# Keys, routing choice, output projection, final norm and gate weights moved beside each other in a two-layer encoder kernel on one core

## The reference, cut to what matters

```python
mem_n = rms_norm(mem, mem_norm)
for i in range(2):
    h = rms_norm(x, norm_mix[i])
    mkv = mem_n @ w_mem_kv[i]            # 1024 x 512: keys 0:256, values 256:512
    # i = 0: neighbourhood attention; i = 1: chunked gated linear attention (GLA),
    # whose decay gates come from gla_gate_up and whose output is normed by gla_out_norm
    mix, mq = ...
    x = x + concat([mix, memory_attention(mq, mkv)]) @ w_out[i]
    # top-1 of 4 groups, then top-2 of its 8 experts, each (silu(h@w1) * (h@w3)) @ w2
    x = x + hierarchical_moe(rms_norm(x, norm_ffn[i]), ...)
return rms_norm(x, final_norm)
```

## Time and profile before

| what | value |
|---|---|
| median of 3 runs | 1174.23 us (1173.82 to 1175.13) |
| the profiled execution | 1174.4 us, of which the span is 1172.6 us |
| PE busy | 875.2 us, 75% of the span |
| DVE / ACT / POOL busy | 225.5 / 181.3 / 18.6 us |
| moved by DMA | 444.06 MB, mean 379 GB/s |
| chain that ended last | PE 54%, DMA 42% |
| costliest line in it | expert weights landing, 40% |

### The profile page before, as it was taken

How to read it: one execution, slowest core, us unless ns; L and a number is a source line. 1 busy time by engine, 2 the same in 40 slices (tenths; PEclk the granted TensorE clock), 3 DMA queues, 4 the chain that set the end, 5 groups by cost and what they waited for, 6 DMA issues and landing times.

```text
span 1172.6 us, 11688 instructions
## 1 busy us (share of the span) xinstructions
PE 875.2 (75%) x5138; PEld 411.9 (35%) x5138; DVE 225.5 (19%) x427; ACT 181.3 (15%) x385; POOL 18.6 (2%) x15
## 2 busy tenths in 40 slices
PE   8999998383976465655999999976475656575676
PEld 7678553131522121211358665422121212121222
DVE  2234342010011010100115453311010101110012
ACT  3233221010000000000035521200000000000002
POOL 1400000000000000000000000000000000000000
PEclk9999999686998887877999999988787878777789
DMA  9985679999999999999999737999999999999997
GB/s 342 256 269 241 222 310 428 429 427 428 418 429 427 427 428 428 426 427 429 414 284 330 274 144 274 427 425 427 429 428 428 429 429 426 428 428 428 428 419 259
DMA packets 89769, 444.06 MB, mean 379 GB/s; under 512 B 36080, under 2 KB 54896, under 8 KB 67056
## 3 DMA queue, kind: packets, MB, share of 16 engines
q1 hardware_dynamic: 88992, 442.04, 93.5%
q10 hardware_dynamic: 720, 1.19, 0.3%
HBM read 442.16 MB, written 1.05 MB: 378 GB/s over the span
## 4 chain that ended last, share of the span: by engine, by line
PE 54%; DMA 42%; issue 1%; DVE 1%; ACT 1%; SPq 0%; DVEq 0%
DMA ring<-in_moe_w 40%; PE ps L847 15%; PE ps L851 9%; PE ps L704 5%; PE ps L1015 4%; PE ps L744 4%; PE ps L833 2%; PE ps L820 2%; PE ps L1099 2%; PE ps L752 1%; PE ps L684 1%; PE ps L697 1%; PE ps L1065 1%; PE ps L736 1%; PE ps L717 1%
## 5 line engine op out<-in xcount | busy, mean ns | idle before, releaser
L847 PE MATMUL ps<-ring,work 128*32 128x512 f32 x2032 | 274.9, 665 | 146.8 <-DMA ring<-in_moe_w 138.7
L851 PE MATMUL ps<-ring,work 128*32 128x512 f32 (+1 forms) x1088 | 141.8, 681 | 107.1 <-DMA ring<-in_moe_w 104.4
L847 PEld LDWEIGHTS ps<-ring,work 128*32 128x32 f32 x2032 | 82.1, 120 | 326.7 <-issue 326.4
L851 PEld LDWEIGHTS ps<-ring,work 128*32 128x32 f32 x1088 | 40.1, 127 | 197.7 <-issue 191.0
L1775 DVE TENSOR_TENSOR xres<-xres,ps 128x512 f32<-128x512 f32 (+1 forms) x68 | 44.6, 657 | 282.2 <-PE ps L820 282.1
L833 PE MATMUL ps<-xs,work 128*128 128x512 f32 x112 | 55.1, 638 | 10.0 <-issue 9.3
L820 PE MATMUL ps<-work 128*128 128x512 f32 (+1 forms) x136 | 59.7, 581 | 1.6 <-ACT work L1368 1.6
L1766 DVE TENSOR_TENSOR work<-work,ps 128x512 f32<-128x512 f32 x16 | 11.0, 688 | 253.2 <-PE ps L847 253.2
L704 PE MATMUL ps<-ring 128*128 128x384 f32 x160 | 53.4, 490 | 0.0
L1380 ACT COPY work<-ps 128x512 f32<-128x512 f32 x28 | 16.4, 586 | 217.8 <-PE ps L851 217.8
L1359 ACT COPY work<-ps 128x256 f32<-128x256 f32 x16 | 6.0, 372 | 268.0 <-PE ps L879 268.0
(11 more groups left out here) (254 smaller groups left out, 692.8 us busy)
## 6 DMA issues: line engine op xcount, KB each, us to landing
ring<-in_moe_w SPq DMA_DIRECT2D x187, 2048.0 KB, 31.5
ring<-in_w_out SPq DMA_DIRECT2D x4, 2048.0 KB, 16.6
ring<-in_na_w_in SPq DMA_DIRECT2D x7, 1024.0 KB, 12.2
ring<-in_gla_w_in SPq DMA_DIRECT2D x4, 1536.0 KB, 10.8
ring<-in_moe_w SPq DMA_DIRECT2D x4, 1024.0 KB, 19.6
ring<-in_moe_w SPq DMA_DIRECT2D x8, 512.0 KB, 11.4
ring<-in_na_w_in SPq DMA_DIRECT2D x1, 3072.0 KB, 19.9
ring<-in_na_rpb SPq DMA_DIRECT2D x12, 192.0 KB, 5.7
```

What stands on the lines that cost most here:

```text
L847: return pe.matmul(ps[32 * e:32 * e + 32, 4 + m, :], xsel[:, k, 32 * e:32 * e + 32], w, start=k == 0, stop=k == KC - 1, tile_position=(0, ...
L851: return pe.matmul(ps[32 * e:32 * e + 32, bank, 0:w.shape[-1]], actT[:, j, 32 * e:32 * e + 32], w, start=j == 0, stop=j == 3, tile_positio ...
```

## The change

- Layer 1's keys: their 1 MB of weights (`kw1`) is loaded by SP ahead of fill 6 of layer 0 into `work`; `mem_k(1)` runs inside quad 0 of layer 0, between the w3 products and the transposes; ACT keeps the result in `kTm1_kept` ahead of quad 0's sigmoid, and copies it to its place at quad 3. The values stay at quad 3, with a 1 MB load.
- The gates' weights go into the part of `wlog` that layer 0's logits have used, and are loaded ahead of fill 11 of layer 0; the output norm is loaded in the seam, behind w_out.
- Choice: the triangle carries -1024 on its diagonal and the ramp starts at -1024, so that `place` compares the count in PSUM itself. Both `keep_warm` matmuls stand behind L785.
- w_out of layer 1 lies in the ring as two halves by columns, not by rows, and tile 1 goes through its first half first. Slot 6 is released after that.
- The final norm's row is read once, and two matmuls with a row of ones spread it at quad 4 of layer 1.
- At the start the keys' weights come in two DMAs by halves of the rows, with a wait for each, and the memory's scaling waits for its own gain only. In the seam `vw1[0]` comes in two such halves.
- `within(0)` runs ahead of the last memory head's product.

```diff
-KV_AT = 3
+KV_AT, FNORM_AT = 3, 4
...
+CHOSEN = 1024.0
...
-    c[:, C_TRI:C_TRI + P] = np.triu(np.ones((P, P)), 1)
+    c[:, C_TRI:C_TRI + P] = np.triu(np.ones((P, P)), 1) - CHOSEN * np.eye(P)
...
-    c[:, C_IOTAM:C_IOTAM + 32] = np.arange(32) - 64
+    c[:, C_IOTAM:C_IOTAM + 32] = np.arange(32) - CHOSEN
...
-        gup = cut(ring, 10 * SLOT + 3520, 2 * DK)
+        gup = wlog[:, 0].rearrange("p k n -> p (k n)")[:, 0:2 * DK]
...
+        kw1 = cut(work, KEPT, KC, 256)
+        kTm1_kept = cut(work, 1696, MPAIR, T)
...
-        wow = [[region(0, 0, D, 4), region(6, 0, D, 4)], [region(6, 0, D, 4), region(4, 0, D, 4)]]
+        wow = [[region(0, 0, D, 4), region(6, 0, D, 4)], [region(6, 0, HALF_D, KC), region(4, 0, HALF_D, KC)]]
...
-                 2: (g_mm, 2 * TT), 7: (ring_used, B1 + 8), 10: (m_tr, 1), 8: (m_tr, 2), EXTRA: (o_mix, 2), 4: (ring_used, PRE1), 6: (ring_used, PRE1 - 1),
+                 2: (g_mm, 2 * TT), 7: (ring_used, B1 + 8), 10: (m_tr, 1), 8: (m_tr, 2), EXTRA: (o_mix, 2), 4: (ring_used, PRE1), 6: (wo_half, 2),
...
-                        sp.dma_start(kvw[1], rows(w_mem_kv[1], 0, 512)).then_inc(ring_in[kv_slot], 16)
-                        sp.wait_ge(s_gup0, 1)
-                        for dst, src in gate_loads():
-                            sp.dma_start(dst, src).then_inc(s_gate, 16)
+                        sp.dma_start(kvw[1], rows(w_mem_kv[1], 256, 512)).then_inc(ring_in[kv_slot], 16)
...
+                        if l == 0 and g == 0 and main[0].slots[f] == 7:
+                            sp.wait_ge(at_tr, N1)
+                            sp.wait_ge(s_memT, 1)
+                            sp.dma_start(kw1, rows(w_mem_kv[1], 0, 256)).then_inc(ring_in[EXTRA], 16)
+                        if l == 0 and g == 0 and f == FILLS - 1:
+                            sp.wait_ge(s_gup0, 1)
+                            for dst, src in gate_loads():
+                                sp.dma_start(dst, src).then_inc(s_gate, 16)
                         free(l, n0 + f)
...
-            sp.dma_start(kvw[0][:, :, 0:256], rows(w_mem_kv[0], 0, 256)).then_inc(ring_in[0], 16)
+            for half in range(2):
+                k = slice(4 * half, 4 * half + 4)
+                sp.dma_start(kvw[0][:, k, 0:256], rows(w_mem_kv[0], 0, 256)[:, k, :]).then_inc(ring_in[(8, 0)[half]], 16)
...
-            sp.dma_start(vw1[0][:, :, 0:HALF], chunk_rows(win1, MIX, MIX + HALF)).then_inc(ring_in[6], 16)
-            sp.dma_start(vw1[0][:, :, HALF:WIDE], chunk_rows(win1, 3 * MIX, 3 * MIX + 32)).then_inc(ring_in[6], 16)
+            for half in range(2):
+                k, there = slice(4 * half, 4 * half + 4), ring_in[(EXTRA, 6)[half]]
+                sp.dma_start(vw1[0][:, k, 0:HALF], chunk_rows(win1, MIX, MIX + HALF)[:, k, :]).then_inc(there, 16)
+                sp.dma_start(vw1[0][:, k, HALF:WIDE], chunk_rows(win1, 3 * MIX, 3 * MIX + 32)[:, k, :]).then_inc(there, 16)
...
+            sp.dma_start(gnorm, gla_out_norm[0:1, :].to_broadcast([P, DV])).then_inc(s_gate, 16)
...
-            pool.wait_ge(ring_used, PRE0 + 1)
+            pool.wait_ge(first.sel_ready, 1)
             nc.gpsimd.memset(gup, 0.0).then_inc(s_gup0, 1)
...
+            def mem_k(l):
+
...
+                w = kvw[0] if l == 0 else kw1
                 if l == 0:
-                    arrived(landed_kv0)
+                    arrived(landed_kv0[0])
                 else:
-                    slot, there = main[0].fill(0, KV_AT * FILLS)
-                    pe.wait_ge(ring_in[slot], there)
+                    arrived(landed_k1)
                     pe.wait_ge(s_memT, 1)
                 for k0 in (0, 4):
                     if l == 0 and k0 == 4:
+                        arrived(landed_kv0[1])
                         pe.wait_ge(n_hTa, TT)
                     for m in range(MPAIR):
                         for k in range(k0, k0 + 4):
-                            t = pe.matmul(ps[:, KVB[l], m * T:(m + 1) * T], w[:, k, m * P:(m + 1) * P], memT[:, k, :],
+                            t = pe.matmul(ps[:, KB[l], m * T:(m + 1) * T], w[:, k, m * P:(m + 1) * P], memT[:, k, :],
                                           start=(m, k) == (0, 0), stop=(m, k) == (MPAIR - 1, KC - 1))
                 t.then_inc(kv_mm, 1)
+
+            def mem_v(l):
...
+            def mem_v(l):
+
+                w = kvw[0][:, :, 256:512] if l == 0 else kvw[1]
...
+                else:
+                    slot, there = main[0].fill(0, KV_AT * FILLS)
+                    pe.wait_ge(ring_in[slot], there)
...
+            def out_rows(l, c, half):
+
+                if l == 0:
+                    return wow[0][c // 4][:, c % 4, HALF_D * half:HALF_D * half + HALF_D]
+                return wow[1][half][:, c, :]
...
-                keep_warm(1, NBANK[2 * l + 2][1])
+                keep_warm(2, NBANK[2 * l + 2][1])
...
-                keep_warm(2, NBANK[i][1])
                 positions1(l)
...
+                if pick_count is None and l == 0:
+                    mem_k(1)
                 pe.wait_ge(rn.sig.sel_ready, sel_count + 1)
                 for a in range(TT):
                     t = pe.transpose(ps[:, 2, a * P:(a + 1) * P], selw[:, a].rearrange("p e s -> p (e s)"), ident)
                 t.then_inc(rn.sig.selT_mm, 1)
+                if pick_count is None and l == 0:
+                    pe.wait_ge(kv_cp, 3 + 1)
                 pe.wait_ge(rn.sig.act_ready, c + 1)
...
-                        mem_kv(1)
-                        pe.wait_ge(kv_cp, 3 + 2)
+                        mem_v(1)
+                        pe.wait_ge(kv_cp, 3 + 3)
+                    if l == 1 and g == FNORM_AT:
+                        pe.wait_ge(s_fn, 16)
+                        for half in range(2):
+                            t = pe.matmul(ps[:, 2 + half, :], ones[0:1, :], fnorm[0:1, half * 512:half * 512 + 512],
+                                          start=True, stop=True)
+                        t.then_inc(s_fn, 1)
+                        pe.wait_ge(s_fn, 16 + 3)
...
-            arrived(landed_v1[0])
+            arrived(landed_v1[0][0])
             for a in range(TT):
                 for k in range(KC):
+                    if (a, k) == (0, 4):
+                        arrived(landed_v1[0][1])
...
             probs_T(N1 + 1, prob1)
+            pe.wait_ge(q_in, 2)
+            pe.wait_ge(k_in, 2)
...
+            within(0)
             pe.wait_ge(at_oT, N1 + 1)
             weighted(N1 + 1, pT1, v_mem(1, 1))
...
-            out_proj(1, 1, (0,), 5)
+            out_half(1, 0, (0, 1))
             pe.wait_ge(res[1], 1)
             transpose_tile(4, xres, 0, NBANK[4][0])
-            out_proj(1, 1, (1,), 5)
+            out_half(1, 0, (2, 3))
             logits(1, 0, range(KC))
-            out_half(1, 0, (2, 3, 4, 5)).then_inc(wo_half, 1)
+            out_half(1, 0, (4, 5)).then_inc(wo_half, 1)
+            out_half(1, 1, (0, 1))
             positions0(1)
-            second_half_of_tile1(1, (2, 3), True)
+            second_half_of_tile1(1, (2, 3))
...
-                act_e.wait_ge(kv_mm, l + 1)
-                nc.scalar.copy(kTm[l].rearrange("p m t -> p (m t)"), ps[:, KVB[l], :]).then_inc(kv_cp, 1)
                 act_e.wait_ge(ring_used, main[0].used(0, KV_AT * FILLS + 1))
-                nc.scalar.copy(vm[l].rearrange("p a n -> p (a n)"), ps[:, KVB[l] + 1, :]).then_inc(kv_cp, 1)
+                nc.scalar.copy(vm[l].rearrange("p a n -> p (a n)"), ps[:, VB[l], :]).then_inc(kv_cp, 1)
+                act_e.wait_ge(kv_cp, 3 + 1)
+                nc.scalar.copy(kTm[l], kTm1_kept).then_inc(kv_cp, 1)
+
+            def keep_k1():
+
+                act_e.wait_ge(kv_mm, 2)
+                act_e.wait_ge(first.sel_ready, 2)
+                nc.scalar.copy(kTm1_kept.rearrange("p m t -> p (m t)"), ps[:, KB[1], :]).then_inc(kv_cp, 1)
...
+                if pick_count is None and c == 0:
+                    keep_k1()
...
-                        act_e.dma_start(fnorm, final_norm.rearrange("(o d) -> o d", o=1).to_broadcast([P, D])).then_inc(s_fn, 16)
+                        act_e.dma_start(fnorm[0:1, :], final_norm.rearrange("(o d) -> o d", o=1)).then_inc(s_fn, 16)
+                    if l == 1 and g == FNORM_AT:
+                        act_e.wait_ge(s_fn, 16 + 1)
+                        for half in range(2):
+                            nc.scalar.copy(fnorm[:, half * 512:half * 512 + 512], ps[:, 2 + half, :]).then_inc(s_fn, 1)
...
-                dve.wait_ge(rt_m, 2 * l + a + 1)
-                link(V.tensor_scalar(t32a[:, a, :], msk[:, a, :], -1000.0, 1000.0, ALU.mult, ALU.add))
                 dve.wait_ge(rt_p, 3 * l + a + 1)
-                link(V.tensor_tensor(ppos[:, a, 0:NE], t32a[:, a, :], ps[:, POSB[l], a * NE:(a + 1) * NE], ALU.add))
-                V.tensor_tensor(sel[:, a], iota.unsqueeze(1).to_broadcast([P, E4, CAP]),
-                                ppos[:, a, 0:E4].unsqueeze(2).to_broadcast([P, E4, CAP]), ALU.is_equal).then_inc(done, 1)
```

(18 more changed lines are left out.)

74 lines of the change are left out of this document (31 added, 43 removed).

## The result

The changed kernel takes 1164.98 us (median of 4 runs, 1164.55 to 1165.24), the kernel before, on the same chip, 1174.29 us: ratio 0.9916, 95% interval 0.9904 to 0.9929. That is faster by 9.3 us by the medians and by 9.85 us by the two profiled executions (1174.4 and 1164.55). The forecast was 1163.4 us in a range of 1161.3 to 1167.3: the time lies in the range, 1.6 us above the forecast and 0.7 above the range's middle. Measured a second time, the same kernel took 1165.07 us, ratio 0.9921 (0.9907 to 0.9934).

What follows compares the result with a forecast made beforehand. Full DMA queues were taken to bound the expert stretches, PE the rest. Seven terms summed to 10.85 us off the profiled 1174.4, giving 1163.55, and 1163.4 us with the median 0.17 below; range 1161.3 to 1167.3.

Steps and rivals of the forecast that it cites:

- start: At the kernel's start, keys loaded in two halves let the keys' product begin at 8.3: 1.35 us earlier (bounds 0, 1.6).
- choice, layer 0: In layer 0's choice, PE reaches the mask's matmul 0.86 earlier and an addition leaves the path: 1.1 us (0.2 to 1.2).
- keys and gates out of the stretch: In layer 0's expert stretch, landings around the values' load come 7.8 apart instead of 11.3: 3.5 us saved (2.4 to 3.9).
- V's weights in halves: In the seam, the first half's earlier landing lets PE start the V product when ready: 0.6 us (bounds 0, 0.6).
- `within` earlier: In the seam, `within(0)` fills PE's wait of 1.2 for ACT's copy: 1.0 us gained (bound 0).
- layer 1: choice and slot 6: At layer 1's first fills, choice gives 1.1 and an earlier fill 9 gives 1.0 more: 2.1 us (1.1 to 3.3).
- final norm's row: In layer 1's full stretch, 512 KB less to move: 1.2 us saved (bounds 1.0, 1.3).
- Quad 0: In layer 0's quad 0, added keys' work delays releases to 196.0 and 213.0, hidden by a 5.0 us margin before 201.0.
- Gate loads blocking SP: Rival ahead of layer 0's fill 11: eight issues at 1.0 each make that fill 1.9 late, 1165.3 us; chance 0.13.
- Halves buying nothing: Rival at start and seam: both keep waiting for the whole load, so 1.35 and 0.6 are missing, 1165.4 us; chance 0.14.
- Dry queue: Rival in layer 0's quad 0: late releases run the DMA queue dry, 1172.9 us or slower than before; chance 0.04.
- More than summed: Rival: slot 6's early fill in layer 1 brings all 3.3 and the start 1.6, 1162 us; chance 0.09.

Runs made afterwards that it cites:

- idle-matmul run: The changed kernel with 16 idle matmuls of 512 columns added behind the second layer's keys' product in quad 0 of layer 0; 1171.10 us, ratio 0.9963.

## Why the prediction was right, and where it was off

The mechanism held in the main: the stretches are bound by bytes, and work outside them shifts all that follows. That the gains add held everywhere but in layer 1's two edits. The steps by their sizes:

| term | predicted | by the lead | by undoing it |
|---|---|---|---|
| start | 1.35 | 1.0 | 1.1 |
| choice, layer 0 | 1.1 | 1.1 | 1.1 |
| keys and gates out of the stretch | 3.5 | 2.6 | 1.7 and 0.7 |
| gate loads ahead of fill 11 | 0 | 0 | |
| V's weights in halves | 0.6 | 0.9 | 0.9 |
| `within` earlier | 1.0 | 0.9 | 0.9 |
| layer 1: choice and slot 6 | 2.1 | 1.7, in the second profile 0.3 | 0.6 to 0.8 for either, 0.8 for both |
| final norm's row | 1.2 | 1.3 | 1.3 |

- **Keys and gates** hold 0.9 us of what was missing (1.6 by the medians, 1.0 by the first profile). The mis-sized number is the fill beside the load, left at "4.92": the values' load itself takes 2.8 to 3.0, near the 2.9 that was taken, but a fill next to it takes 0.6 to 1.0 more, as one did beside the 2 MB load before, and that share doesn't go when the load is halved. So the stay of the values' load is 3.8, not 2.9. The two landings were said to be 7.8 apart; they are 300.00 - 292.27 = 7.7 in the first profile, by luck, since there the fill ahead had paid the surplus, and 8.8 in the second. The sum has to be taken over the whole stay of the load, from 286.42 on.
- **Start.** "I put its end at 8.3" was DVE's scaling; it ended at 8.62, since PE's transposes of the second tile ended at 7.9. The product then waited for that and not for a half. The first half landed at 7.85, as put (8.0).
- **V's weights.** Bounded at 0.6 by PE being ready then; the product itself also took 11.18 instead of 11.44 us.
- **Layer 1** is the larger miss on the mean: 0.8 us instead of 2.1, below its lower bound of 1.1. The choice gave its 1.1 at the issue of fill 12, and "fill 12 finds the queue empty" was near enough (fill 11 landed 3.0 us after fill 12's issue, at 736.92). But the landing on that empty queue was taken as 8.2 after the issue, and it came 8.7 to 10.2 after it, mean 9.6, later than the 9.2 in the full queue before. So the "1.0 more" was a loss of some 0.4. That the first profile shows 1.7 is luck of the draw.
- **Quad 0** was released at 196.56 (196.0) and again at 213.38 (213.0), with no hole, and that closeness is in part luck. The serial work ahead of the w2 products came as summed: 10.25 us for 10.3 (before they started at 179.78, which is 177.7 less the lead of 2.1; now at 187.93). But the prediction shifted quad 0 by the choice's 1.1 alone and left out the start's gain, which makes it 1.0 us too late, and it took the clock as full, which makes it 1.5 too early. The idle-matmul run shows that the margin was 3.0 us, not 5.0: the deadline had been taken at 201.0 with the same gain left out (fill 17 landed at 203.2, not 204.3).
- **Rivals.** Gate loads blocking SP: no, 1.8 us to spare. Halves buying nothing: no, in both places. Dry queue: not reached, though PE's clock fell for a while. "More than summed": no.

## What to carry to other kernels

Where a queue of large loads is the bound, price a foreign load by its whole stay (from the last undisturbed landing to the next one), not by its bytes: here 1 MB cost 3.8 us, 2 MB 5.5, eight loads of 6 KB 0.7, and for the 1 MB it made no difference whether SP or ACT issued it. An edit that opens a hole in the queue pays up to the next release only; look for what releases the next load before adding its gain, and where two edits meet at one load, undo each alone and compare with both undone before summing them. Work that is moved into a covered place can lower PE's clock by the wait behind it; read the clock there before calling it free. And where single edits are worth 1 us and executions differ by 2, compare two traces event by event, and profile the same kernel twice before reading a step of under 2 us.

## What the runs showed that I had not expected

- The first landing behind a partly empty queue took 8.7 to 10.2 us in twelve profiles of nearly the same code, 8.8 and 10.2 in two of the same kernel. Where the queue was full, landings repeat to 0.1 us, except beside the values' load (3.6 to 4.0 for its stay).
- At the seam PE's granted clock fell to 0.57 and 0.61 over 4 us behind gaps of 1.6 and 0.8 us in two profiles of thirteen, and stayed at 1.00 in the rest; it cost 1.65 us. In quad 0 it fell in all eleven profiles with the keys there and no idle matmuls, behind waits of some 3.9 and 0.7 us.
- Two edits at layer 1's fill 12, each next to nothing alone as far as one profile of each shows, gave 0.8 us together on the mean.
- A 2 MB load at full width cost 5.5 us among fills of 2 MB that cost 4.9, the surplus in the fill behind it; a 1 MB load in 1 KB rows took 2.9 itself and 0.6 to 1.0 of a neighbour, where half a fill's time is 2.45.
